# First stage of a two-layer decoder trunk: how x is transposed, scaled and split before the first matrix products

## The reference

```python
def rms_norm(x, g):
    y = x * rsqrt(mean(x * x, axis=-1) + 1e-5)
    return y * g
def swiglu(x, w_gate, w_up, w_down):
    return (silu(x @ w_gate) * (x @ w_up)) @ w_down
h = x
h = h + 0.5 * swiglu(rms_norm(h, ln_ffn1[0]), ffn1_w_gate[0], ffn1_w_up[0], ffn1_w_down[0])
```

## Time and profile before

| | us |
|---|---|
| median of 3 executions | 927.67 |
| lowest, highest | 927.12, 927.94 |
| the profiled execution | 927.52 |
| its span in the trace | 925.7 |
| TensorE busy in the span | 916.2 |
| VectorE, ScalarE, GpSimd busy | 565.5, 468.3, 95.7 |
| first product of the kernel starts | 7.84 |
| second column chunk starts | 20.25 |

### The profile page before, as it was taken

The page is one execution under the profiler, slowest core; times in us unless marked ns, Lnnn a source line. Parts: engine busy times, 40 slices in busy tenths (PEclk is TensorE's granted clock), DMA queues, the critical chain, the costliest instruction groups (busy, mean ns, idle before and its releaser), DMA issues.

```text
span 925.7 us, 11565 instructions
## 1 busy us (share of the span) xinstructions
PE 916.2 (99%) x4259; PEld 753.0 (81%) x4259; DVE 565.5 (61%) x597; ACT 468.3 (51%) x620; POOL 95.7 (10%) x172
## 2 busy tenths in 40 slices
PE   9999999999999999999999999999999999999997
PEld 7888888888877888888888888888876788888885
DVE  5666663663487766665467666654578675766542
ACT  6545543565685645444445545433458554444431
POOL 1000006534311100000003000000030010000000
PEclk9999999999999999999999999999999999999999
DMA  9898777555432688876557788875473187987621
GB/s 311 260 282 249 228 255 226 182 194 215 182 96 87 221 265 259 252 258 223 185 175 239 240 249 250 302 241 176 143 267 98 46 274 242 277 250 285 225 83 46
DMA packets 162557, 197.61 MB, mean 213 GB/s; under 512 B 14360, under 2 KB 133216, under 8 KB 162512
## 3 DMA queue, kind: packets, MB, share of 16 engines
q1 hardware_dynamic: 161552, 196.12, 65.0%
q0 software_dynamic: 512, 0.36, 0.4%
q10 hardware_dynamic: 448, 0.53, 0.2%
HBM read 181.77 MB, written 15.20 MB: 213 GB/s over the span
## 4 chain that ended last, share of the span: by engine, by line
PE 97%; issue 1%; DMA 1%; DVE 0%; ACT 0%; SPq 0%; POOL 0%; POOLq 0%; ACTq 0%
PE bank L485 60%; PE bank L522 20%; PE bank L526 10%; PE bank L542 2%; PE bank L706 1%; PE bank L579 1%; PE bank L759 1%; PE bank L681 1%; PE bank L737 1%; DMA raw<-in_ffn_w_up 1%; PE bank L699 1%; DVE x L1758 0%; SPq L1026 0%; ACT junk L1337 0%; SPq L1113 0%
## 5 line engine op out<-in xcount | busy, mean ns | idle before, releaser
L1698 DVE TENSOR_TENSOR w_lo<-raw,w_hi 128x2048 fp32r<-128x2048 f32 x154 | 351.6, 2292 | 189.7 <-ACT w_hi L1318 189.4
L1318 ACT ACTIVATE w_hi<-raw 128x2048 fp32r<-128x2048 f32 x154 | 295.0, 1918 | 201.9 <-PE bank L526 106.2
L485 PE MATMUL bank<-w_hi,xT_hi 128*128 128x512 f32 x816 | 319.5, 391 | 0.0
L485 PE MATMUL bank<-w_hi,xT_lo 128*128 128x512 f32 x816 | 317.9, 390 | 0.0
L485 PE MATMUL bank<-w_lo,xT_hi 128*128 128x512 f32 x816 | 317.8, 389 | 0.0
L485 PEld LDWEIGHTS bank<-w_hi,xT_hi 128*128 128x128 f32 x816 | 153.3, 188 | 32.7 <-issue 0.7
L485 PEld LDWEIGHTS bank<-w_hi,xT_lo 128*128 128x128 f32 x816 | 153.2, 188 | 31.9
L485 PEld LDWEIGHTS bank<-w_lo,xT_hi 128*128 128x128 f32 x816 | 153.3, 188 | 31.2
L522 PE MATMUL bank<-w_hi,hT_hi 128*128 128x512 f32 x348 | 135.8, 390 | 0.0
L522 PE MATMUL bank<-w_lo,hT_hi 128*128 128x512 f32 x348 | 135.5, 389 | 0.0
L526 PE MATMUL bank<-w_hi,hT_lo 128*128 128x512 f32 x348 | 107.2, 389 | 0.0
(11 more groups left out here) (181 smaller groups left out, 599.2 us busy)
## 6 DMA issues: line engine op xcount, KB each, us to landing
raw<-in_ffn_w_down SPq DMA_DIRECT2D x88, 512.0 KB, 5.4
raw<-in_ffn_w_gate SPq DMA_DIRECT2D x86, 512.0 KB, 5.4
raw<-in_ffn_w_up SPq DMA_DIRECT2D x86, 512.0 KB, 6.7
raw<-in_a_w_qkv SPq DMA_DIRECT2D x24, 512.0 KB, 5.4
h_bounce<-silu SPq DMA_DIRECT2D x40, 256.0 KB, 6.8
xn<-h_bounce SPq DMA_DIRECT2D x160, 64.0 KB, 3.1
raw<-in_a_w_o SPq DMA_DIRECT2D x8, 512.0 KB, 3.7
raw<-in_b_w_q SPq DMA_DIRECT2D x8, 512.0 KB, 5.3
```

What stands on the lines that cost most here:

```text
L485: mm = nc.tensor.matmul(bank[b][:, :], xs[:, kt, own(pos)], ws[:, slot(u), cols], start=(kt == 0 and i == 0), stop=(kt == KT - 1 and i == 2))
L1318: nc.scalar.activation(w_parts(u)[0], raw[:, slot(u), :], ACT.Copy).then_inc(s_hi, 1)
L1698: nc.vector.tensor_tensor(lo, raw[:, slot(u), :], hi.bitcast(F32), ALU.subtract).then_inc(s_lo, 1)
```

## The change

The first stage treats x in pieces of two tiles. Piece i of a position is tiles 2i and 2i+1; pieces 0 and 2 of a position share one bank and pieces 1 and 3 the other. VectorE's multiplication into xn is gone: ScalarE reads each tile of a piece from the bank, scales it by the gain column and writes xT_hi (two 128x128 instructions for a piece), and VectorE makes xT_lo from the bank in the same way (two `scalar_tensor_tensor`). TensorE waits for a piece at every even tile. Both pieces of x half (0,0) are transposed first, with 14 warm transposes behind them; the transposes of pos 1's first half come after the products of tiles 0 and 1 of pos 0, the others further on, and from tile 4 the two positions alternate. Weight tiles 2 and 3 are loaded by separate transfers, ahead of x's second halves.

```diff
-        FIRST_PARTS = [(0, 1), (1, 2), (2, 4), (4, 6), (6, 8)]
+        FIRST_PIECES = [(0, 0), (0, 1), (1, 0), (1, 1), (0, 2), (0, 3), (1, 2), (1, 3)]
+        def piece_bank(pos, i):
+            return x_banks(pos)[i % 2]
+        FIRST_PARTS = [(0, 1), (1, 2), (2, 3), (3, 4), (4, 6), (6, 8)]
...
-                    if k == 0:
-                        pe.wait_ge(s_first_lo, first_halves().index((pos, u)) + 1)
+                    if kt % 2 == 0:
+                        in_sbuf(pe, ("xT", "ln_ffn1_0", pos, kt // 2))
...
-                    for kt in range(3):
-                        first_tile(kt, 0)
-                    half_transposes(0, 1)
-                    half_transposes(1, 1)
-                    for kt in range(3):
-                        first_tile(kt, 1)
+                    first_tile(0, 0)
+                    first_tile(1, 0)
+                    piece_transposes(1, 0)
+                    piece_transposes(1, 1)
+                    first_tile(0, 1)
+                    first_tile(1, 1)
+                    first_tile(2, 0)
+                    first_tile(2, 1)
+                    piece_transposes(0, 2)
+                    piece_transposes(0, 3)
                     first_tile(3, 0)
                     first_tile(3, 1)
-                    for pos in range(NPOS):
-                        for kt in range(4, 7):
+                    piece_transposes(1, 2)
+                    piece_transposes(1, 3)
+                    for kt in range(4, 7):
+                        for pos in range(NPOS):
                             first_tile(kt, pos)
...
-            half_transposes(0, 0)
-            warm(8)
-            half_transposes(1, 0)
-            warm(4)
+            def piece_transposes(pos, i):
+                pe.wait_ge(s_x[2 * pos + i // 2], 16)
+                transposes([x[:, pos, P * kt:P * (kt + 1)] for kt in (2 * i, 2 * i + 1)], piece_bank(pos, i),
+                           ("xT", "ln_ffn1_0", pos, i))
+            piece_transposes(0, 0)
+            piece_transposes(0, 1)
+            warm(14)
...
-                    if i == 2:
+                    if i == 3:
                         load_x(0, 1)
                         load_x(1, 1)
...
+            def first_hi(pos, i):
+                act.wait_ge(s_filled, filled["xT", "ln_ffn1_0", pos, i])
+                for kt in (2 * i, 2 * i + 1):
+                    ins = nc.scalar.activation(xT_hi[:, kt, own(pos)], bank[piece_bank(pos, i)][:, P * (kt % 2):P * (kt % 2 + 1)],
+                                               ACT.Copy, scale=first[:, kt:kt + 1])
+                ins.then_inc(s_first_hi, 1)
+            act.wait_ge(s_first, 1)
+            first_hi(0, 0)
             first_split(0)
-            first_hi(0, 0)
             first_split(1)
+            first_hi(0, 1)
+            first_hi(1, 0)
             first_split(2)
-            first_hi(1, 0)
+            first_hi(1, 1)
             first_split(3)
+            first_hi(0, 2)
             first_split(4)
-            first_hi(0, 1)
+            first_hi(0, 3)
+            first_hi(1, 2)
             first_split(5)
+            first_hi(1, 3)
             first_split(6)
-            first_hi(1, 1)
             first_split(7)
...
+            def first_lo(pos, i):
+                dve.wait_ge(s_first_hi, FIRST_PIECES.index((pos, i)) + 1)
+                b = piece_bank(pos, i)
+                for kt in (2 * i, 2 * i + 1):
+                    ins = nc.vector.scalar_tensor_tensor(out=xT_lo[:, kt, own(pos)], in0=bank[b][:, P * (kt % 2):P * (kt % 2 + 1)],
+                                                         scalar=first[:, kt:kt + 1],
+                                                         in1=xT_hi[:, kt, own(pos)].bitcast(F32),
+                                                         op0=ALU.mult, op1=ALU.subtract)
+                ins.then_inc(s_read[b], 1)
```

More of the change, by code:

```diff
@@ L237, in trunk @@
         s_raw = [sem(f"s_raw{i}") for i in range(UNITS_HELD)]
-        s_part = [sem(f"s_part{i}") for i in range(3)]
+        s_part = [sem(f"s_part{i}") for i in range(4)]
         s_part_hi = sem("s_part_hi")
@@ L242, in trunk @@
         s_first = sem("s_first")
-        s_first_lo = sem("s_first_lo")
+        s_first_hi = sem("s_first_hi")
         s_vec = [sem(f"s_vec{i}") for i in range(VEC_RING)]
@@ L435, in tile_of @@
             return view[:, kt // 4, BANK * (kt % 4):BANK * (kt % 4 + 1)]
-        def first_halves():
-            return [(0, 0), (1, 0), (0, 1), (1, 1)]
-        FIRST_PARTS = [(0, 1), (1, 2), (2, 4), (4, 6), (6, 8)]
+        FIRST_PIECES = [(0, 0), (0, 1), (1, 0), (1, 1), (0, 2), (0, 3), (1, 2), (1, 3)]
+        def piece_bank(pos, i):
+            return x_banks(pos)[i % 2]
+        FIRST_PARTS = [(0, 1), (1, 2), (2, 3), (3, 4), (4, 6), (6, 8)]
         def first_full(i):
-            return (s_part[0], s_part[1], s_raw[0], s_part[2], s_raw[1])[i]
+            return (s_part[0], s_part[1], s_part[2], s_raw[0], s_part[3], s_raw[1])[i]
         @block.tensor
@@ L856, in _ @@
             warm(3)
-            def half_transposes(pos, j):
-                pe.wait_ge(s_x[2 * pos + j], 16)
-                transposes(tiles(x[:, pos, :], j), x_banks(pos)[j], ("xT", "ln_ffn1_0", pos, j))
-            half_transposes(0, 0)
-            warm(8)
-            half_transposes(1, 0)
-            warm(4)
+            def piece_transposes(pos, i):
[5 more added lines that the diff above has]
+            warm(14)
             ffn(0, U_FFN1_0, "ln_ffn1_0", "ln_mix_0")
@@ L2011, in _ @@
             dve.wait_ge(s_first, 1)
-            first_gained(0, 0)
+            first_lo(0, 0)
             first_split(0)
-            first_lo(0, 0)
             first_split(1)
-            first_gained(1, 0)
+            first_lo(0, 1)
+            first_lo(1, 0)
             first_split(2)
-            first_lo(1, 0)
+            first_lo(1, 1)
             first_split(3)
-            first_gained(0, 1)
+            first_lo(0, 2)
             first_split(4)
-            first_lo(0, 1)
+            first_lo(0, 3)
+            first_lo(1, 2)
             first_split(5)
-            first_gained(1, 1)
+            first_lo(1, 3)
             first_split(6)
-            first_lo(1, 1)
             first_split(7)
```

## The result

The changed kernel takes 930.58 us (median of 7 executions, 930.51 to 930.80), the kernel before beside it 927.94 (7 executions, 927.12 to 928.35). The ratio is 1.0031, 95% interval 1.0022 to 1.0041: slower by 2.6 us, or 0.3%. The profiled execution took 930.51.

The account below looks back on a forecast made before the run. TensorE, busy 99% of a 925.7 us span, bounds the kernel. An earlier start, a stand and unit 2's late split move the second chunk from 20.25 to 22.88; 927.67 + 2.6 = 930.3, range 929.2 to 932.0.

Parts of the forecast that it names:

- part 1: At the first product: fewer warm transposes let it start at 7.60 instead of 7.84, a gain of 0.24 us.
- Part 2: Before the product (tile 0, rows 1): TensorE stands about 1.35 us until the moved transposes are converted; product at 10.86.
- the sign: In the changed profile: a TensorE wait of 1.2 to 1.5 before (tile 0, rows 1), near 9.5 to 10.9.
- The small instructions: ScalarE's 128x128 passes from a bank: 0.27 us apart, 0.37 for the last; sixteen replace four, 2.2 us more.
- Part 3: Rest of the first stage: ScalarE starts unit 2's split at 18.59 instead of 15.92; second chunk at 22.88.
- The weights decide, by 0.7: At the first stage's end: unit 2's splits put the second chunk at 22.88, TensorE's own queue only at 22.14.
- Costed at nothing: First-stage effects given no time of their own, among them VectorE's passes and SP's two more issues ahead of unit 2.
- these DMAs would be what is late next: Loads of unit 2 and x's second halves: late next, by up to 0.9 us, if ScalarE's delay were gone.
- A: Rival, not slower: pieces are converted before TensorE asks, unit 2's landing holds the end at 20.2; 927.7; 8%.
- B: Rival, the clock: after its stand TensorE falls to 1.2 GHz, products 0.45 apart, 2.9 us more; 933.2; 8%.
- C: Rival at the stage's end: TensorE's queue decides, not the weights; +1.6, 929.3; low end of the 84% own case.

Follow-up runs that it names:

- the run with the arithmetic alone: The kernel before with only direct bank reads by ScalarE and VectorE (four 128x128 instructions each per half), VectorE's multiplication into xn gone: 927.61, ratio 1.0000.
- the run with halves: The changed kernel with unit 2 of the weights split by ScalarE and VectorE in two halves of two tiles: 929.75, ratio 1.0019.
- the run with the transfers alone: The kernel before with only weight tiles 2 and 3 in separate transfers, x's second halves behind the fourth part: 928.23, ratio 1.0007.
- the one with all pieces ahead: The changed kernel with rows 1's first transposes before the first product, table load early, x's second-half pieces transposed together before tile 2: 927.92, ratio 1.0000.
- rows 1 ahead: The changed kernel with the transposes of rows 1's first half (pieces (1,0) and (1,1)) ahead of the first product again: 928.97, ratio 1.0016.

## Why the prediction was right, point by point

The forecast was 930.3, +2.6, slower; measured 930.58, +2.64. The medians agree better than the two profiles do, where the second chunk moved by 3.02. The profiled execution of before was 0.42 under its median of seven, that of the changed kernel 0.07 under its own. That the medians agree to within 0.1 us is therefore luck: the sum left out 0.48 at the start (part 1), and it set out from a 20.25 that was early by about as much. By the difference of 907.3 in the table above, an estimate, a median execution of before has its second chunk at 20.6. The path and its largest terms were right, apart from the start.

- **Part 1, the start: wrong.** "What it needs is there: hi and lo of piece (rows 0, tiles 0-1) and weight tile 0 are done by about 6.7." The last of them, the lo part of weight tile 0, ended at 7.94, because the table load of 1.28 us, over by 3.5 in the kernel before, came at 4.68. The first product started at 8.08, not 7.60, and that was 0.24 lost instead of 0.24 gained. The run with the load early gives its price: 1.12 in the second chunk, 0.6 to 0.9 in the median. The prediction had no term for it. Without the load the start would have come sooner than I thought, at 6.96, as the warm transposes ran faster than I had assumed: the fourteen took 2.16 from their first start to the product, 0.15 each, where my 7.60 came to 0.20 each. The row of the load stands in the trace of before; I took its place as fixed.
- **Part 2, the stand: right.** From the start of the four transposes to the product behind them I had 1.80 (9.06 to 10.86); it took 1.74 (9.54 to 11.28). The recorded idle time is 1.14 against 1.35, since it is counted from the modelled end of the transposes; this puts it just under the 1.2 to 1.5 that I had named as the sign. With the transposes moved back ahead the second chunk came 1.63 earlier.
- **The small instructions: right.** ScalarE's are 0.26 apart (two in 0.63, four in 1.13 to 1.14, the last 0.37), for which I had taken 0.27 by the 256-column row. The run with the arithmetic alone shows no cost in the total: what the small instructions take more fell into ScalarE's idle time. The Trainium skill, "VectorE: DVE Perf Modes", section "The TRN2 errata", gives 172 + columns cycles at 1.2 GHz for a bank source, by which the estimate for 128 columns was 0.25; the 0.26 of the trace agrees. The Trainium skill's advice there, tiles of at least 512 elements, points at the arithmetic as the cause; the run with the arithmetic alone doesn't bear that out for this kernel.
- **Part 3, who sets the end: right.** ScalarE had its last run from 16.39 to 18.97, 2.58 against 2.67; unit 2's two splits and hand-over took 4.30 against 4.29. From first product to second chunk I had 15.28, measured 15.19. "The weights decide, by 0.7": 0.65 by the run with halves.
- **Costed at nothing.** SP's two issues cost nothing in this kernel, as said; that "these DMAs would be what is late next, by up to the 0.9" was borne out at 0.5 in the run with the transfers alone and 0.3 in the one with all pieces ahead. Unit 2's issue started at 7.52 against 7.07, so two issues more made it 0.45 later and not 0.9.
- **Rivals.** A's floor was right (with the order mended the time is that of before, held by unit 2's landing), its premise didn't occur. B didn't occur: the products behind the 1.14 us stand go on 0.23 apart. C didn't occur: the weights decided.

Against the profile, then, the forecast shift of 2.6 was 0.4 short: 0.48 too little at the first product (the table load), 0.09 too much behind it.

## What to carry to other kernels

An in-order queue turns "do the ready products first" into a stand if the next instruction in it needs the full trip through two other engines; put what feeds a trip ahead by at least its length (here 1.7 us for two tiles). Look up where one-off costs such as a table load stand relative to the first wait: moving a wait ahead of an engine's first instruction can put them on the path. And before costing smaller instructions, see whether their engine idles: 2.2 us more on ScalarE was free here.

## What the runs showed of the hardware

- The load of the activation table comes in front of the first activation, and either ahead of that activation's wait or behind it: at 2.23 to 2.25 in the kernels whose first activation is a weight split or the constant's copy, with one wait, and at 4.67 to 4.68 in those whose first activation reads the transposed piece behind two waits. It took 1.28 us each time. Whether the number of waits decides its place, no run varied alone.
- The pace of the first transposes changes from execution to execution. Eight warm ones from 4.80 took 1.91 us in the kernel before and 1.04 in the one with the arithmetic alone; fourteen took 2.43 in the changed kernel. By the starts, they go from 0.21 apart to 0.10 to 0.12 apart somewhere between 4.8 and 7.4 us. The granted clock reads 1.00, the 2.4 GHz level, in the earlier trace rows all the same, so the profile doesn't show why. Where the table load comes at 4.67, the first product starts at 8.07 or 8.08 whatever the pace; in the other kernels it starts anywhere from 6.96 to 8.10.
- This shows in the spread. Executions of the changed kernel lie within 0.3 us, with unit 2 in halves within 0.14, with rows 1 ahead within 0.36, all three with the table load on the path; with the load early they spread over 1.2 (929.33 to 930.52), and the seven of the kernel before over 1.2; the other kernels without the load on the path spread over 0.65 to 1.6. A path through ScalarE and VectorE seems to hide how the transfers and the pace of the transposes vary. That is an inference from the ranges; no run varied it alone.
